# A streaming encoder layer on one core: input weights prepared with one scale per 128-column tile, the norm vector applied to the rows, earlier loads

## The reference

```python
h = rmsnorm(x, norm_g)                    # x * rsqrt(mean(x*x) + 1e-6) * norm_g
u = h @ w_in                              # w_in is 1024 x 2816: 11 splits of 256 columns
a_b, a_c, a_x, a_g, b_v, b_a, b_g, c_u, c_g, x_q, x_g = split(u, 11)
# A: a_b * conv3(a_c * a_x) * silu(a_g)
# B: silu(layernorm(conv31(b_v * sigmoid(b_a)))) * silu(b_g)
# C: (trailing means of c_u over 2/4/8/16, minus c_u) @ pool_w, bias, scale, * silu(c_g)
# X: softmax(x_q @ mem_k.T / 8) @ mem_v * silu(x_g)   # 256 memory tokens
# mem_k, mem_v = rmsnorm(mem, mem_norm_g) @ w_mem_k, ... @ w_mem_v
y = rmsnorm(x + concat(A, B, C, X) @ w_out, final_norm_g)
```

## Time and profile before

| | |
|---|---|
| runs | 1681.28, 1681.56, 1682.69 us; median 1681.56 |
| profiled execution | span 1680.8 us, the only time it gives; 0.8 us under the median |
| busy | PE 1532.9 (91%), DVE 1361.0 (81%), ACT 681.1 (41%), POOL 284.4 (17%) |
| chain that ended last | PE 64%, DVE 23%, issue 9%, ACT 3% |
| mean granted TensorE clock | 0.975 |

### The profile page before, as it was taken

How to read it: one execution, slowest core, us unless ns; L and a number is a source line. 1 busy time by engine, 2 the same in 40 slices (tenths; PEclk the granted TensorE clock), 3 DMA queues, 4 the chain that set the end, 5 groups by cost and what they waited for, 6 DMA issues and landing times.

```text
span 1680.8 us, 34281 instructions
## 1 busy us (share of the span) xinstructions
PE 1532.9 (91%) x12307; PEld 1326.6 (79%) x12307; DVE 1361.0 (81%) x3363; ACT 681.1 (41%) x1367; POOL 284.4 (17%) x208
## 2 busy tenths in 40 slices
PE   2663699999999999999999999999999999999986
PEld 1553588888888888888888888888888888888875
DVE  6799969787787879696978878796979787787867
ACT  3433353434344343534343433434352434344344
POOL 4476211111111001111111111010111111110010
PEclk9977799999999999999999999999999999999998
DMA  7700042222222040322222221303122222213024
GB/s 203 188 13 1 20 145 95 82 75 88 88 78 98 26 150 19 107 69 82 86 77 88 88 88 45 131 19 123 53 82 94 73 84 88 88 64 106 20 73 140
DMA packets 80678, 140.00 MB, mean 83 GB/s; under 512 B 7098, under 2 KB 32894, under 8 KB 80574
## 3 DMA queue, kind: packets, MB, share of 16 engines
q1 hardware_dynamic: 80573, 138.96, 25.2%
HBM read 121.27 MB, written 17.66 MB: 83 GB/s over the span
## 4 chain that ended last, share of the span: by engine, by line
PE 64%; DVE 23%; issue 9%; ACT 3%; DVEq 0%; DMA 0%; SPq 0%; ACTq 0%
PE u L408 13%; PE u L410 13%; PE u L409 13%; DVE z L1037 7%; PE qps L408 4%; PE qps L410 4%; PE qps L409 4%; PE sps L408 3%; PE sps L410 2%; PE sps L409 2%; PE qps L484 2%; DVE wo_lo L988 1%; DVE gf L1009 1%; DVE st L964 1%; DVE h_lo L984 1%
## 5 line engine op out<-in xcount | busy, mean ns | idle before, releaser
L408 PE MATMUL u<-h_hi,w_hi 128*128 128x256 f16 (+1 forms) x2992 | 791.2, 270 | 1.3 <-issue 0.8
L409 PE MATMUL u<-h_lo,w_hi 128*128 128x256 f16 (+1 forms) x2992 | 790.1, 270 | 0.0
L410 PE MATMUL u<-h_hi,w_lo 128*128 128x256 f16 (+1 forms) x2992 | 790.0, 270 | 0.0
L1037 DVE SCALAR_TENSOR_TENSOR z<-glu,cst,z 128x256 f32<-128x256 f32 (+1 forms) x1020 | 424.7, 487 | 0.0
L408 PEld LDWEIGHTS u<-h_hi,w_hi 128*128 128x128 f16 x2992 | 293.9, 99 | 44.0 <-issue 5.6
L410 PEld LDWEIGHTS u<-h_hi,w_lo 128*128 128x128 f16 x2992 | 294.0, 99 | 33.2
L409 PEld LDWEIGHTS u<-h_lo,w_hi 128*128 128x128 f16 x2992 | 294.2, 99 | 32.4
L693 ACT ACTIVATE gate<-u,inv 128x256 f32<-128x256 f32 (+1 forms) x204 | 83.6, 461 | 219.5 <-PE u L410 219.4
L988 DVE TENSOR_TENSOR wo_lo<-stage,wo_hi 128x512 fp32r<-128x512 f32 x136 | 100.1, 764 | 47.1 <-ACT wo_hi L716 47.1
L1397 POOL TENSOR_TENSOR sa<-cu 128x540 f32<-128x540 f32 (+1 forms) x17 | 30.6, 1800 | 627.5 <-ACT cu L693 627.5
L408 PE MATMUL sps<-wo_hi,y_hi 128*128 128x512 f32 (+1 forms) x280 | 113.9, 407 | 12.3 <-DVE y_lo L1075 6.5
(11 more groups left out here) (191 smaller groups left out, 2352.4 us busy)
## 6 DMA issues: line engine op xcount, KB each, us to landing
stage<-in_w_out SPq DMA_DIRECT2D x136, 256.0 KB, 5.1
ob<-in_x_prompt SPq DMA_DIRECT2D x34, 512.0 KB, 3.9
probs<-in_w_out SPq DMA_DIRECT2D x68, 256.0 KB, 3.1
out<-ob SPq DMA_DIRECT2D x32, 512.0 KB, 3.1
xb<-in_x_prompt SPq DMA_DIRECT2D x30, 512.0 KB, 4.2
sb<-in_w_out SPq DMA_DIRECT2D x34, 256.0 KB, 3.9
sa<-in_w_out SPq DMA_DIRECT2D x34, 256.0 KB, 3.4
w_hi<-in_w_in SPq DMA_DIRECT2D x10, 512.0 KB, 6.7
```

The lines of the kernel that those rows point to most:

```text
L408: nc.tensor.matmul(out, a_hi, b_hi, start=first, stop=False)
L409: nc.tensor.matmul(out, a_hi, b_lo, start=False, stop=False)
L410: return nc.tensor.matmul(out, a_lo, b_hi, start=False, stop=last)
L1037: ins = nc.vector.scalar_tensor_tensor(z[:, c, 0:n], glu[:, c, k:k + n], w, z[:, c, 0:n], ALU.mult, ALU.add)
```

## The change

The norm vector no longer goes into the weights: it is broadcast to all partitions (`gx`), scaled once by a power of two (`gain_scale`), and `rows_scale` multiplies by it as a full tensor instead of by a constant. The memory's rows do the same with `gm`. A weight tile gets one scale, from the sum of its squares: ACT squares and sums (`w_squares`), PE adds over partitions in one small product on top of a tiny constant, DVE does three instructions on two columns, ACT takes the high part with that scale, and DVE takes the low part of both tiles with the scale inside. POOL does nothing for the weights. gf has memory of its own and is loaded early; the memory's products move from behind split 0 to behind split 2; `AHEAD` is 3; splits 5 to 9 are loaded before memory weights 4 to 7. The memory that SBUF needs for this comes from the DMA scratch area, cut to 1024 bytes per partition.

```diff
-AHEAD, GAINS = 4, 5
+AHEAD = 3
@@ SP, start
+            sp.dma_start(gx[:, :], norm_g[0].partition_broadcast(P)).then_inc(gx_in.sem, 16)
             load_split(0)
+            sp.dma_start(ob[:, 1, :], x_prompt[0, P:2 * P, :]).then_inc(first_in[1].sem, 16)
+            load_split(1)
...
+            sp.dma_start(gm[:, :], mem_norm_g[0].partition_broadcast(P)).then_inc(gm_in.sem, 16)
+            load_split(2)
+            load_split(3)
...
+            load_split(4)
...
+            for g in range(5, NG - 1):
+                load_split(g)
+            sp.dma_start(gf[:, :], final_norm_g.partition_broadcast(P)).then_inc(gf_in.sem, 16)
+            sp.wait_ge(mt_ready.sem, 2)
+            sp.dma_start(xb[:, :], x_prompt[0, 2 * P:3 * P, :]).then_inc(x_in.sem, 16)
             for k in range(4, KT):
                 load_memory_weights(k)
+            sp.wait_ge(kw_lo.sem, KT)
+            load_split(NG - 1)
@@ PE, weight_sums
-                for k in range(KT):
-                    ins = nc.tensor.matmul(bank[:, 0:CT * P], ones[:, :], mags[:, :, k, :], start=k == 0, stop=k == KT - 1)
+                nc.tensor.matmul(bank[:, 0:CT], ones[:, :], tiny[:, :], start=True, stop=False)
+                pe.wait_ge(wsq_ok.sem, CT * (g + 1))
+                nc.tensor.matmul(bank[:, 0:CT], ones[:, :], w_sq[:, CT * g:CT * g + CT], start=False,
+                                 stop=True).then_inc(u_ready.sem, 1)
@@ ACT
+            def w_squares(g):
...
+                    nc.scalar.activation(junkw[:, j % 2, :], w_flat(j), ACT.Square, accum_out=w_sq[:, j:j + 1]).then_inc(wsq_ok.sem, 1)
+            def w_high(g):
...
+                    nc.scalar.activation(w_hi[:, j], w_raw(j), ACT.Copy, scale=w_scl[:, j:j + 1]).then_inc(whi_ok.sem, 1)
@@ DVE, rows_scale, w_scale (all that was there goes), w_low
-                nc.vector.tensor_scalar(rows[0:m, :], rows[0:m, :], X_Y[0:m, 0:1], factor, ALU.mult, ALU.mult).then_inc(x_scaled.sem, 1)
+                nc.vector.scalar_tensor_tensor(rows[0:m, :], rows[0:m, :], X_Y[0:m, 0:1], gain[0:m, :],
+                                               ALU.mult, ALU.mult).then_inc(x_scaled.sem, 1)
+                nc.vector.tensor_scalar(w_exp[:, o].bitcast(I32), bank[:, 0:CT].bitcast(I32), 1, EXP_MASK,
+                                        ALU.logical_shift_right, ALU.bitwise_and).then_inc(wscl_ok.sem, 1)
...
+                for j in (CT * g, CT * g + 1):
...
+                    nc.vector.scalar_tensor_tensor(w_lo[:, j].rearrange("p k c -> p (k c)"), w_flat(j), w_scl[:, j:j + 1],
+                                                   w_hi[:, j].rearrange("p k c -> p (k c)"),
+                                                   ALU.mult, ALU.subtract).then_inc(wlo_ok.sem, 1)
@@ DVE, before chunk 0
+            rows_rms(0, P)
+            gain_scale()
+            rows_scale(0, P, gx, ob[:, 0])
...
+            w_scale(0)
+            rows_lo(0, ("t2", "t3"), 2, 1, P)
+            w_low(0)
+            w_scale(1)
```

More of the change, by code:

```diff
@@ L602, in chunk @@
                     weight_sums(AHEAD - 1)
+                    weight_sums(AHEAD)
+                    memory_transposes(0, xb)
+                    memory_transposes(1, ob[:, 0])
+                prj("b_v")
+                prj("x_q")
+                if first:
                     memory_products()
-                    weight_sums(AHEAD)
-                prj("b_v")
+                prj("c_u")
                 if first:
                     keys_t(0)
-                prj("x_q")
-                prj("c_u")
-                if first:
                     pe.wait_ge(kt_l.sem, 1)
@@ L823, in chunk @@
                 if first:
+                    memory_hi(0)
+                    memory_hi(1)
+                    for k in range(4):
+                        kw(k)
+                prepare(1)
+                if nxt:
+                    squares(nxt[0][1], nxt[0][3], i)
+                scaled_out(i, n, "x_q", dq_hi[:, :, 0:n], ACT.Copy, q_hi)
+                prepare(2)
+                if first:
+                    for k in range(4, KT):
+                        kw(k)
+                    act.wait_ge(pw_in.sem, 64)
+                    nc.scalar.activation(pw_hi[:, :, :], ya[:, 0, :].rearrange("p (c m) -> p c m", c=CT), ACT.Copy).then_inc(pw_ok.sem, 1)
                     act.wait_ge(kvp.sem, KT)
                     nc.scalar.activation(kv[:, :, :], sps[:, :, :], ACT.Copy).then_inc(kv_ok.sem, 2)
[L826 to L832, removed]
[L833 to L835 removed]
                 act.wait_ge(hist_ok.sem, hist_ok.at(i, 3))
@@ L840, in chunk @@
                 prepare(3)
+                if first:
+                    keys_values_hi(0)
                 exps(i, n, 0)
@@ L1134, in chunk @@
                 prepare(2)
-                prepare(3)
-                taps(i, n, 6, 11)
+                if first:
+                    for k in range(4, KT):
+                        kw(k)
+                        taps(i, n, k + 2, k + 3)
+                    dve.wait_ge(pw_ok.sem, 1)
+                    nc.vector.tensor_tensor(pw_lo[:, :, :], ya[:, 0, :].rearrange("p (c m) -> p c m", c=CT),
+                                            pw_hi[:, :, :].bitcast(F32), ALU.subtract).then_inc(pw_ok.sem, 1)
+                    prepare(3)
+                    keys_values_lo(0)
+                    taps(i, n, 10, 11)
+                else:
+                    taps(i, n, 6, 11)
                 softmax_max(i, n, 0)
                 if nxt:
-                    rows_scale(nxt[0][0], nxt[0][2], XSCALE)
+                    rows_scale(nxt[0][0], nxt[0][2])
                 taps(i, n, 11, 12)
@@ L1241, in chunk @@
                     if q == KT + 5 and len(nxt) > 1:
[L1242 removed]
+                        rows_scale(nxt[1][0], nxt[1][2])
                     if q == KT + 3:
```

290 lines of the change are left out of this document (99 added, 191 removed).

## The result

The changed kernel takes **1626.7 us** in the median of four runs (1624.3 to 1629.7); the kernel before, run beside it on the same chip, takes 1681.5. The ratio is 0.967 (95% interval 0.966 to 0.968), 54.8 us less. The forecast was 1620.5 us, with 1601 to 1641 as its range. Every run lies 2.1 us above its span. The profiled execution has a span of 1625.2 us, against 1680.8 before: 55.6 us less.

The account below looks back on a forecast made before the run. DVE, slowed by POOL, was taken to bound the first 219 us, PE the loop. From the profiled 1680.8 us, minus 69 for chunk 0 plus 8 for the loop gave 1619.8, as median 1620.5 us; range 1601 to 1641.

Parts of the forecast that it names:

- DVE's work in chunk 0: DVE's busy time up to chunk 0's out_half: falls from 186.8 to 109 us.
- DVE's idle time: Named waits of DVE before chunk 0's out_half: together 41 us, putting out_half near 150 us.
- the walk: Chunk 0's new order stepped through with measured durations: out_half near 150 us, gain 69; chance 60 in 100, spread 1608 to 1635.
- rival 1: Chunk 0: DVE is slowed by something that stays, not POOL; stretching of 27 us returns, 1648; chance 4 in 100.
- The 27 us: Stretching of DVE in chunk 0 laid to POOL: taps 8.5, L964 and L966 10.5, other DVE work 8.
- the 52.1 us: DVE's time before out_half for making the per-column powers of two, all counted as saved.
- rows_scale in the loop: Second input adds 0.53 us before the softmax division PE waits for; 15 chunks, +8 us.
- The upper bound of 20 us: Loop cost of rows_scale if 0.84 us more stretching comes on top of 0.53: 1.4 per chunk, 20 us.
- rival 2: Start: loads decide, at 249 GB/s the rows of chunk 1 land at 66 us, 11 later; 1632; chance 13.
- rival 3: Chunk 0: gaps close, half the idle time behind the start goes (13 us or more); 1604; chance 15.
- Rival 4: Loop: rows_scale and POOL's window sums shut each other out, 80 us lost, 1692; decides from 4.6 us per chunk; chance 3.
- Rival 5: Chunk 0: weights still decide, DVE stands for ACT, idle time as in the upper bound; 1660; chance 5.

Follow-up runs that it names:

- the one without the gain: Changed kernel with every chunk's rows_scale (rows of chunk 1 and later) again a tensor_scalar over one tensor, norm-vector multiplication left out; 1615.4 us.

## Why the prediction was right

The forecast lies 6.2 us under the result, and the terms show where: 3.0 us in chunk 0 (66.0 measured for 69), 2.4 behind it (10.4 for 8), and 0.8 because the median lies 1.5 us above the profiled span and not 0.7.

- **DVE's work in chunk 0.** Predicted 109 us, measured 109.0. By group: scales 5 against 6.2, low parts 28.2 against 28.1, taps 25.2 against 24.7, one-column steps 8.6 against 8.6. The last agreement is luck: 42 steps ran in place of 39, half of them (L969) take 0.16 us and not 0.22, and one L967 took 1.28 beside a product on POOL.
- **DVE's idle time.** Predicted 41 us, measured 44.5, out_half at 153.5 in place of 150. The gaps were those of the walk: high part of split 1 (4 predicted, 3.1, and 1.1 for that of split 2), glu (4, 4.5), rows of chunk 1 (3, 5.3), split 5 (8, 10.5), split 6 (4, 4.6). The largest misses are the rows of chunk 1, which landed at 56.7 in place of 55, and split 5; start, first rows and tail together were shorter than thought, 15.4 against 18. First product: 21 predicted, 21.9 measured.

  The walk had the memory's products end near 74 us, and they ended at 76.9. It left out TensorE's clock, which fell while PE stood 12.0 us for the low parts of their weights (windows of PE alone, columns as above):

```profile
68.60:74.30 5.70, 5.64 (x13) 0.50 0.03 9
74.60:76.90 2.30, 2.30 (x11) 1.00 1.09 316
```

  At the lower clock PE's timeline has three of the products in 1.28 us, at the higher one in 0.69, so the thirteen lost some 2.6 us (an estimate from these). DVE stood for split 5 behind them; what a higher clock alone would be worth there, no run shows.
- **The cause of the stretching (rival 1).** It was POOL. The 27 us that I put it at were too low as its whole size. In the kernel before, the operations that I booked under scales and wide passes were stretched as well:

```profile
L1009 DVE SCALAR_TENSOR_TENSOR gf<-gf,ident x22: 277/286/2466, 28.6 to 191.4; 128x128 f32<-128x128 f32 x22
```

At its median of 0.286 us L1009 would cost 6.3 us and not 25.3. By this the 52.1 us were for a good part stretching, which the prediction counted as the scales' own cost; no run takes POOL's work alone out of the kernel before. The sum came out since these operations were removed with their measured, stretched times.
- **rows_scale in the loop.** Predicted +0.53 a chunk and 8 us, measured 7.6 for the wait itself; 1.28 us shortest, 2.14 longest, chunk 92.4, as forecast. PE's wait is 1.9 us in 11 of the 15 chunks and 1.6 to 1.7 in four. In three of these four POOL's window sum stretched the taps behind rows_scale instead.
- **The step that was short.** The sum for the loop took PE's wait as the whole price. It left out that PE, having stood longer, at times goes on at its lower clock: 3.2 us in the profiled run. The upper bound of 20 us held it, for another reason.
- **Rivals.** The loads (rival 2) land where the walk had them, within 2 us; the gap behind them could be filled by order alone. The gaps did not close by themselves (rival 3), though with other orders two of them do. Rival 4 needed 4.6 us a chunk and got 10.4 / 15 = 0.7, the clock included. Rival 5 had 82 us of idle time, and 44.5 were there. The walk's own spread, written as 1608 to 1635, is 1610 to 1634 by its terms.

The base was fair: the sum starts from the span of the profiled execution and adds 0.8 us to reach the median. A run's time lies 2.1 us above its own span, so that execution was 1.4 us slower than the median run.

## What to carry to other kernels

Before adding an input to an operation on DVE, read what it stands in front of: here 0.5 us ahead of a division that PE waits for in 15 chunks cost 11 us, and the same operation in a gap of DVE left no wait of PE behind it. If a wait is taken out of one place of a queue, price the next customer of that queue as well; with rows_scale just behind the division, 0.8 of the 1.3 us that it gained came back. Work on POOL that nobody waits for is not free while DVE is the bound; here 1 us of it made DVE's work 0.57 us longer (40.5 for 71).

## What the runs showed of the hardware that I had not expected

TensorE's granted clock can fall to 1.2 GHz behind a short stand in the middle of dense work. With waits of up to 1.4 us no chunk showed it (14 chunks each of the kernel before and of the one without the gain). With 1.9 us it was 6 chunks in 70 (two in the changed kernel, one each in four others), with 3.1 us 10 in 14. Each time it lasted some 3 us and cost 1.5 or 1.6. In all 16 of these chunks the trace shows a granted clock of 0.50 over 3.2 us. What decides in which chunk it falls stays open; the length of the wait raises how often.

When POOL and DVE meet, the stretched operation changes from chunk to chunk. These are two neighbouring chunks of the changed kernel, DVE's timeline:

```profile
295.02 2.13 DVE L979 SCALAR_TENSOR_TENSOR xb<-xb,st,gx 128x1024 f32<-128x1024 f32 x1
297.07 1.71 DVE L1041 SCALAR_TENSOR_TENSOR z<-glu,cst,z 128x256 f32<-128x256 f32 x2
...
387.43 1.28 DVE L979 SCALAR_TENSOR_TENSOR xb<-xb,st,gx 128x1024 f32<-128x1024 f32 x1
388.62 2.08 DVE L1041 SCALAR_TENSOR_TENSOR z<-glu,cst,z 128x256 f32<-128x256 f32 x2
```

The two taps take 0.88 us undisturbed. In the first chunk rows_scale pays 0.85 and the taps 0.83, in the second the taps alone pay 1.2. POOL's window sum starts 0.02 or 0.03 us ahead of rows_scale in both; it takes 1.08 us in the first, where rows_scale is held, and 2.24 in the second, where it is not. The maximum of one line would not tell the price.
